# Half of eight gate tiles' products moved from the input projection into the opening of the delta scan

## What is computed

```python
h = rms_norm(x, lw['norm1_g']) * (1.0 + sc1) + sh1
aq, ak, av, dq, dk_, dv_, dz, dbeta, dalpha, ga, gb = jnp.split(h @ lw['w_in'], split_idx, axis=-1)
...
qkv = short_conv(jnp.concatenate([dq, dk_, dv_], axis=-1), conv_w)
...
t_inv = lax.linalg.triangular_solve(eye + lmat, jnp.broadcast_to(eye, lmat.shape),
                                    left_side=True, lower=True, unit_diagonal=True)
...
v_new = u_i - jnp.einsum('bhcd,bhde->bhce', w_i, state)
...
merged = jax.nn.sigmoid(ga) * (o_a @ lw['w_pa']) + jax.nn.sigmoid(gb) * (o_d @ lw['w_pb'])
```

## Time and profile before

| what | us |
|---|---|
| median of 3 runs | 2715.23 |
| lowest and highest | 2710.26, 2716.74 |
| the profiled execution | 2707.89 |
| its span, first to last instruction | 2706.1 |
| PE busy (matmul) | 2518.4 (93%) |
| VectorE busy | 1721.3 (64%) |
| ACT busy | 1241.5 (46%) |
| POOL busy | 623.8 (23%) |

### The profile page before, as it was taken

The page is one execution under the profiler, slowest core; times in us unless marked ns, Lnnn a source line. Parts: engine busy times, 40 slices in busy tenths (PEclk is TensorE's granted clock), DMA queues, the critical chain, the costliest instruction groups (busy, mean ns, idle before and its releaser), DMA issues. The chain is left out here.

```text
span 2706.1 us, 45790 instructions
## 1 busy us (share of the span) xinstructions
PE 2518.4 (93%) x17286; PEld 2369.3 (88%) x17286; DVE 1721.3 (64%) x2820; ACT 1241.5 (46%) x2235; POOL 623.8 (23%) x558
## 2 busy tenths in 40 slices
PE   6999999969999999985999988989999999999999
PEld 3899899958888888884778778989999999999999
DVE  3666233236676776656898883447886654777776
ACT  4322454324433443315788883344653333555453
POOL 1000222343343433314554453332000000000000
PEclk9999999969999999876999998999999999999999
DMA  5122676443333433205011004643335552537764
GB/s 221 63 87 85 198 247 231 175 119 103 93 97 106 119 107 86 71 25 175 22 42 61 18 13 162 225 145 111 108 108 186 182 178 71 177 108 249 256 229 150
DMA packets 236880, 352.39 MB, mean 130 GB/s; under 512 B 85856, under 2 KB 159616, under 8 KB 235392
## 3 DMA queue, kind: packets, MB, share of 16 engines
q1 hardware_dynamic: 233792, 333.87, 37.4%
q10 hardware_dynamic: 2880, 15.73, 1.7%
HBM read 262.66 MB, written 86.85 MB: 129 GB/s over the span
## 5 line engine op out<-in xcount | busy, mean ns | idle before, releaser
L279 PE MATMUL proj_ps<-h_hi,w_hi 128*128 128x320 f32 x896 | 282.9, 316 | 6.0 <-DVE w_lo L597 5.6
L279 PE MATMUL proj_ps<-h_lo,w_hi 128*128 128x320 f32 x896 | 278.2, 310 | 0.0
L279 PE MATMUL proj_ps<-h_hi,w_lo 128*128 128x320 f32 x896 | 277.9, 310 | 0.0
L1092 ACT ACTIVATE x_inv<-banks_bc 128x1024 fp32r<-128x1024 f32 x120 | 122.5, 1025 | 260.1 <-PE banks_bc L1226 259.0
L2287 DVE TENSOR_TENSOR mf_up_slots<-mf_up_raw,mf_up_slots 128x512 fp32r<-128x512 f32 x198 | 137.3, 693 | 115.8 <-ACT mf_up_slots L2262 115.4
L279 PEld LDWEIGHTS proj_ps<-h_hi,w_hi 128*128 128x128 f32 x896 | 169.6, 189 | 7.1 <-DVE w_lo L597 3.3
L279 PEld LDWEIGHTS proj_ps<-h_lo,w_hi 128*128 128x128 f32 x896 | 169.6, 189 | 0.0
L279 PEld LDWEIGHTS proj_ps<-h_hi,w_lo 128*128 128x128 f32 x896 | 169.4, 189 | 0.0
L3060 PE MATMUL f_ps_b<-mf_t_r,mf_up_slots 128*128 128x320 f32 x1056 | 166.0, 309 | 3.2 <-DVE mf_sg L2975 3.2
L3060 PE MATMUL f_ps_b<-mf_t_s,mf_up_slots 128*128 128x320 f32 x1056 | 165.7, 309 | 2.0 <-PEq L2292 2.0
L3060 PE MATMUL f_ps_c<-mf_t_s,mf_up_slots 128*128 128x320 f32 x1056 | 165.6, 309 | 0.0
(11 more groups left out here) (396 smaller groups left out, 6901.6 us busy)
## 6 DMA issues: line engine op xcount, KB each, us to landing
mf_up_raw<-w_up_dram SPq DMA_DIRECT2D x33, 1024.0 KB, 4.8
w_raw<-w_in_dram SPq DMA_DIRECT2D x58, 512.0 KB, 4.1
mf_down_raw<-down_sums SPq DMA_DIRECT2D x32, 704.0 KB, 4.1
mf_down_raw<-w_down_dram SPq DMA_DIRECT2D x24, 704.0 KB, 4.0
w_ada_raw<-w_ada_dram SPq DMA_DIRECT2D x16, 1024.0 KB, 5.1
mf_w_raw<-w_mix_dram SPq DMA_DIRECT2D x30, 512.0 KB, 5.0
f_t<-mf_c SPq DMA_DIRECT2D x44, 320.0 KB, 2.3
proj_t<-proj_stage SPq DMA_DIRECT2D x32, 320.0 KB, 2.8
```

The lines of the kernel that those rows point to most:

```text
L279: ins = nc.tensor.matmul(out, w(k), a(k), start=(first and n == 0 and q == 0), stop=(last and n == len(ks) - 1 and q == 2))
L1092: nc.scalar.activation(XX[:, c].rearrange("p t h i -> p t (h i)"), BC[c][:], ACT.Copy).then_inc(e["x_ready"], 1)
```

## The change

The second halves of the last eight tiles (m = 12 to 19 of the 20) are no longer computed in the projection but in the scan, in units -3 to -1. The projection ends four steps earlier, at `STEPS_END` = 24. The 16 conditioning units are spread over the 48 groups that are left: split at every third group, products two groups later. `FILLS` is the list of fills, now 28: the eight second halves, then the 20 first halves as before. In the three opening units a slot takes 12 products until the eight are done (32 slots of 39), and 4 in the rest. The eight tiles' 16 groups go in turn to `FB` and to `BC[0][:, 0]`, a bank that units use from unit 0 on, so that a group waits for the evacuation of the one before last.

`h_hi[1]` and `h_lo[1]` must outlive the projection. They move to the top of SBUF (`LATE_HALF`), and buffers of the scan that are first written in unit 0 (`kv`, `XX`, `Y`, `WT`, `S`, `Sd`, `vn`, `kd`, `t1`, `ost`) are laid over them. ACT, VectorE, PE, POOL and SP wait in unit 0 for the sixteenth opening group. The zeroing of the state (4 POOL memsets) goes from the scan's start to unit 0, and the 4 DMAs of `state_in` to unit 1. `load_kv(0)` stands behind `inverse_in(0)`. On ACT, `decay(0)` stands ahead of the first fills.

```diff
-FILL0 = CONV_TILES + ADA2 // 2
-FULL_REST = 6
+FULL_REST, OPEN_TILES = 6, 8
 HALF0 = CONV_TILES + FULL_REST
-FILL_TILES = IN_TILES - HALF0
+HALF_TILES = IN_TILES - HALF0
+STEPS_END = HALF0 + (HALF_TILES - OPEN_TILES) // 2
+PROJ_WEIGHTS = IN_TILES - OPEN_TILES
+FILLS = [(m, 1) for m in range(HALF_TILES - OPEN_TILES, HALF_TILES)] + [(m, 0) for m in range(HALF_TILES)]
+ADA_UNITS = ADA2 // 2
...
+        place = lambda t, g: NG * (t - CONV_TILES) + g
+        ada_split_at = lambda t, g: place(t, g) // 3 if place(t, g) % 3 == 0 else None
+        ada_at = lambda t, g: place(t, g) // 3 if place(t, g) % 3 == 2 else None
+        turn_places = [next(n for n in range(3 * a + 4, 3 * a + 6) if n % NG != NG - 1) for a in range(ADA_UNITS - 1)]
+        ada_turn_at = lambda t, g: turn_places.index(place(t, g)) if place(t, g) in turn_places else None
...
-                if t < LAST:
-                    sp.wait_ge(ada_lo, a + 1)
-                    sp.dma_start(wr[:], io["w_ada"][ADA1 + 2 * a + 2:ADA1 + 2 * a + 4].rearrange("u p k n -> p u k n")).then_inc(ada_in, 16)
-                if t >= HALF0:
-                    load_weight(weight_of(t, 2))
+                for g in range(NG):
+                    if g and new_weight(t, g):
+                        load_weight(weight_of(t, g))
+                    n = ada_split_at(t, g)
+                    if n is not None and n + 1 < ADA_UNITS:
+                        sp.wait_ge(ada_lo, n + 1)
+                        sp.dma_start(wr[:], io["w_ada"][ADA1 + 2 * n + 2:ADA1 + 2 * n + 4].rearrange("u p k n -> p u k n")).then_inc(ada_in, 16)
...
-                rest_hi(weight_of(t) + 1)
-                if a:
-                    ada_out(a - 1)
-                ada_split(a)
                 gate = is_gate(t)
-                for g in range(NG) if gate else (0, 2):
-                    if g and new_weight(t, g):
+                for g in range(NG):
+                    if new_weight(t, g):
                         rest_hi(weight_of(t, g) + 1)
+                    n = ada_split_at(t, g)
+                    if n is not None:
+                        if n:
+                            ada_out(n - 1)
+                        ada_split(n)
...
-                    if g == 1 and a:
-                        ada_turn(a - 1)
-                    if g == 2:
-                        ada(a)
-                        if j is not None:
-                            cols(j, 0)
+                    if ada_turn_at(t, g) is not None:
+                        ada_turn(ada_turn_at(t, g), t)
+                    if ada_at(t, g) is not None:
+                        ada(ada_at(t, g))
+                    if g == 2 and j is not None:
+                        cols(j, 0)
...
+        at_late = [keep["late_half"] - 4096]
+        assert nc.sbuf_base <= at_late[0]
+
+        def late(n, shape, d=F32):
+            t = nc.alloc_sbuf_tensor_at(n, shape, d, offset=at_late[0])
+            at_late[0] += 4 * int(np.prod(shape[1:]))
+            return t
+
+        kv = late("kv_rows", [P, 2, 2, 512])
+        XX = late("x_inv", [P, 2, 2, H4, P], F32R)
...
-        NF, PER = FILL_TILES, 6 * KT
+        NF, PER = len(FILLS), 6 * KT
+        OPEN_GROUPS = 2 * OPEN_TILES
         pieces = {}
         at = [0]
 
         def quota(u):
-            return {-3: 0, -2: 2}.get(u, 4)
+            return 12 if u < 0 and at[0] < PER * OPEN_TILES else 4
+
+        fill_bank = lambda n: BC[0][:, 0] if n < OPEN_GROUPS and n % 2 else FB[:]
...
+                if u == 1:
+                    sp.wait_ge(e["zeroed"], 4)
+                    for d in range(2):
+                        for h in range(2):
+                            sp.dma_start(S[half(h), 1, d, :, h], io["state_in"][d, half(h)]).then_inc(e["state_in"], 16)
...
-                    nc.scalar.activation(fout[:, t % 2, g], FB[:, 0:GN], ACT.Copy).then_inc(e["fill_out"], 1)
+                    nc.scalar.activation(fout[:, t % 2, g], fill_bank(2 * t + g)[:, 0:GN], ACT.Copy).then_inc(e["fill_out"], 1)
...
+                if u == UNITS[0]:
+                    for c in range(2):
+                        decay(0, c)
+                if u == 0:
+                    act.wait_ge(e["fill_ps"], OPEN_GROUPS)
...
-                    if has(u + 3) and lv in (LV[1], LV[2]):
+                    if has(u + 3) and u > UNITS[0] and lv in (LV[1], LV[2]):
...
-                    if lo == 0 and 2 * t + g:
-                        pe.wait_ge(e["fill_out"], 2 * t + g)
+                    n = 2 * t + g
+                    if lo == 0 and n > 1:
+                        pe.wait_ge(e["fill_out"], n - 1 if n < OPEN_GROUPS else n)
                     for i in range(lo, hi):
                         k, part = divmod(i, 3)
                         w = flo if part == 2 else fhi
                         h = h_lo if part == 1 else h_hi
-                        last = mm(FB[:, 0:GN], w[:, t % 2, k], h[:, k, g * GN:(g + 1) * GN], i == 0, i == 3 * KT - 1)
+                        last = mm(fill_bank(n)[:, 0:GN], w[:, t % 2, k], h[FILLS[t][1]][:, k, g * GN:(g + 1) * GN], i == 0, i == 3 * KT - 1)
...
+                    pe.wait_ge(e["fill_out"], OPEN_GROUPS)
+                if u == 1:
...
-                h_hi.append(c1.enter_context(nc.sbuf_tensor("h_hi1", [P, KT, HT], F32R)))
-                h_lo.append(c1.enter_context(nc.sbuf_tensor("h_lo1", [P, KT, HT], F32R)))
+                h_hi.append(nc.alloc_sbuf_tensor_at("h_hi1", [P, KT, HT], F32R, offset=LATE_HALF))
+                h_lo.append(nc.alloc_sbuf_tensor_at("h_lo1", [P, KT, HT], F32R, offset=LATE_HALF + 4 * KT * HT))
```

More of the change, by code:

```diff
@@ L90, in ada_and_norm @@
         mod, mod_s = keep["mod"], keep["mod_scale"]
+        assert nc.sbuf_base <= keep["late_half"]
         block = ctx.enter_context(nc.Block())
@@ L976, in _ @@
                     inverse_in(u + 1)
+                if u == -1:
+                    load_kv(0)
                 if u == 6:
```

82 lines of the change are left out of this document (44 added, 38 removed).

## The result

The changed kernel took 2692.9 us (median of 4 runs, 2688.2 to 2695.2), the kernel before beside it 2716.0 (4 runs, 2710.3 to 2722.4). The ratio is 0.9917 with a 95% interval from 0.9901 to 0.9934: 18 to 27 us faster. Forecast were 2692.0 and a range from 2684 to 2704. The same two kernels measured again later gave 0.9938 (0.9919 to 0.9958), so the two measurements put the gain at 23 and at 17 us.

What follows compares the result with a forecast made beforehand. PE bounds the projection; a latency chain through ACT, VectorE and SP sets the opening, where PE has room. Projection -56.3, opening +32.2, unit 17 +1.0 sum to -23.1 us, from 2715.2 to 2692; range 2684 to 2704.

Steps and rivals of the forecast that it cites:

- Projection, -56.3: Projection's remaining steps: eight tiles times 48 products leave PE's path at 0.147 us each, 56.3 us less.
- Tile 1's wait: Opening: PE waits 2.9 us for tile 1's w_lo, ready 11.3 us after the opening's first product, since ACT has decay(0) first.
- Pace of the tiles: Opening: tiles 1 to 7 take 7.05 us of PE each, with splits and evacuations hidden.
- ACT as pacemaker: Opening: evacuations not hidden, 8.0 us more (2700), or evacuation and split open for seven tiles, 21.4 more (2713); chance 0.20.
- The gate: Opening's end: from ACT's copy of the inverse pair to unit 0, 11.5 us of DMAs and landing.
- VectorE's two microseconds of cover: Opening's end: VectorE's diagonal ends at T+62.4, ACT has evacuated at T+64.4 (T: opening's first product); later delays land on unit 0.
- Second bank, 8.0: Opening: alternating two PSUM banks saves PE's 0.53 us idle at 15 group boundaries, 8.0 us.
- the reading by which the bank saves nothing: Opening: by a Trainium skill rule double-buffering PSUM gains nothing, making the sum -15.1 instead of -23.1; no separate chance given.
- Unit 17, +1.0: Scan, end of the fills: unit 17 gets 48 fills, priced between 0 and 7.0 us, taken as 1.0.
- State loads, 0: Units 0 and 1: moving four state loads and four POOL memsets there costs 0, at worst up to +7.5 us.
- bound for SP's queue, +7.5 at unit 7: Worst case for the moved state loads, from state_out ahead of the diag DMAs, after which unit 7 lasts 36.7 us.
- The half-clock rival: Opening: short waits keep PE at 1.2 GHz, 374 more products cost 0.133 us each, 50 us: 2742; slower has chance 0.05.

Runs made afterwards that it cites:

- the kernel without them: The changed kernel with load_kv(0) back at its old place, early in unit -1: 2699.7 us, ratio 0.9938 to the kernel before.

## Why the prediction was right

Point by point, in its own order:

- **Projection, -56.3.** The opening's first product came 56.2 us earlier. The projection's last product itself came at 490.62, 1.1 us earlier than forecast, because the last conditioning products now stand behind it. PE ran without breaks, and the conditioning kept up; the one trace of its tighter supply is the 0.33 us wait for POOL behind the last product.
- **Tile 1's wait.** Its end was forecast at T+11.3 and came at T+10.7 (1.87 us, forecast 2.9). The cause was the one named, ACT's decay(0) ahead of the split. The slow products came, but later than thought: not the first ten, but two stretches of 3.4 us from 498 and from 508 us.
- **Pace of the tiles.** The sixteenth group's evacuation started at T+65.6, the last product was forecast for T+64.0. No wait for `fill_stage` fell between. ACT as pacemaker, the likeliest rival, is refuted for two banks, and with one bank it is what happened.
- **The gate.** ACT's copy ended at T+66.9 (forecast 65.4); from there to unit 0 it took 11.2 us (11.5). Unit 0 at T+78.1, forecast T+76.9.
- **VectorE's two microseconds of cover.** They were gone, by the mechanism named in brackets: `diag_blocks` behind a 0.5 MB weight load, 3.76 us instead of 2.1. The diagonal ended at T+65.9, forecast T+62.4. It was 3.5 us late and cost nothing only because the forecast's cover of 2.0 and the 1.6 us by which ACT's last evacuation was late itself (done at T+66.0, forecast T+64.4) took it up. Nothing of the cover is left.
- **Second bank, 8.0.** The term for the boundaries was right (8.3), but the whole was under-sized: 14.0. The first boundary, behind decay(0), was missed (4.6). The text held the reading by which the bank saves nothing against its 8.0; that reading is refuted here.
- **Unit 17, +1.0.** 28.7 us against 28.9: nothing. The experiment without fills says why: they hold the clock (1.00 in unit 17 against 0.76 before).
- **State loads, 0.** Units 1 and 2 took 33.2 and 30.4 us against 33.4 and 31.9: nothing is seen of them.
- **The step that failed: unit 0.** The sum has no term for it, and it took 5.0 us more. The text said that `load_kv(0)` had moved behind `inverse_in(0)`, but looked only at what waits ahead of it. Behind it in SP's queue stand the `diag` writes of unit 1, which landed 2.3 us after the last issue instead of 1.1, and behind these, through VectorE's order, unit 0's own products: 1.9 us until the product that reads `y_res`, 3.1 at the lower clock behind it. The prediction's bound for SP's queue, +7.5 at unit 7, was the right kind of row, put to the wrong unit.
- **The half-clock rival** did not come: the opening's clock was 0.95.

Terms worked out: -56.2 + 33.4 + 5.0 - 0.3 = -18.1, against a forecast of -23.1. The medians say -23 and, in the second comparison, -18. The forecast's time was met within 1 us, and that it was met so closely is luck: its sum was 5 us too good by the profiles, and the second comparison's 2698.9 lies 7 us above it.

Two things stay open. Units 5, 7, 10, 14 and 17 take several microseconds more in one execution than in another, at a lower clock where they are longer (unit 5: 31.3 us at 1.00, 33.3 at 0.90); which event starts this was not found. And whether the 5 us of unit 0 are there in the whole kernel's time could not be resolved: the kernel without them measured the same.

## What to carry to other kernels

Work can be moved from a stage where PE is the bound into one where PE waits for a latency chain, and the price is that of the idle time it doesn't fill: read the chain's last link (here copy, DMA out, 16 DMAs, landing) and count which of the moved work stands ahead of it on each engine. When a large load changes its place in a DMA queue, look at the small, dependent transfers *behind* it and at who stands behind their reader. Before taking filler work out of a latency-bound loop, or counting it as a cost, see what the granted clock does without it.

## What the runs showed of the hardware

- Fill products hold TensorE's clock: without them 0.69 instead of 0.98 over 17 units, and 50 us more for 808 matmuls fewer (one run). Unit 17 without fills had 0.76 and 0.61, with 48 of them 1.00.
- Small DMAs behind large ones on the same queue finish late. At the start of unit 0, eight 16x8x16 writes were complete 1.1 us after the last issue behind one 512 KB load or none (six profiles) and 2.3 to 3.3 behind two (five); elsewhere in the scan 1.1 to 3.0 were seen behind one or none, so large loads ahead are not the only cause. A 64 KB load landed after 2.0 to 2.1 us right behind the small writes (23 of 24 cases in twelve profiles) and after 3.4 to 5.0 when a 512 KB load had been issued under 0.7 us before it (45 cases).
- In the changed kernel and its versions with all fills, idle times of PE of 1.5 to 7.1 us ahead of unit 0 and in it were followed by 10 to 34 us at 1.2 GHz, those of 1.9 and 4.8 us at tile 1 by 3.4 us. Where such a stretch falls matters more than that it comes: in unit 0's first part, where VectorE was the later one, it was free (11.2 us at 0.51, 11.0 at 0.98); behind it, 17.8 us at 1.00 became 20.6 to 20.9 at 0.75 to 0.80 and 24.8 at 0.61.
- A first tile run partly at 1.2 GHz cost the opening nothing: it took 1.6 us longer, and PE had to wait for VectorE's `w_lo` behind it in any case (1.9 us, and 4.8 without the slow products).
